# Thirteen matrix products of constants left out of TensorE's queue at three places of a two-block model

## The chip, the cores and the metric

One core of a Trainium2 chip runs one launch of the kernel. The metric is the device time of the launch in microseconds. An execution under the profiler gives the instructions with their times, counted from the first instruction.

## The reference

256 tokens of width 1024 in fp32 pass through a first model of two layers and then a second one of one layer. The first layer is a gated delta rule and a SwiGLU feed-forward; the second layer is an S5 state-space mixer with a gated output (GLU) and a mixture of eight experts, of which each token takes two. Cut to what surrounds the change:

```python
x = layer_norm(ALPHA * x + swiglu(x, ...), ...)          # end of layer 1
u = x @ s5_w_in                                           # entry to the second stage (S5)
...                                                       # state space, gelu
h = val * sigmoid(gate)                                   # halves of hid @ w_glu
x = layer_norm(ALPHA * x + h, ...)
logits = x @ w_router + b_router                          # routing: top 2 of 8
y = sum_e dense_gate[:, e] * swiglu_e(x)                  # experts
x = layer_norm(ALPHA * x + y, ...)
h = rmsnorm(x, norm_mix_g) ; proj = h @ w_in_2            # entry to the second block
```

## The kernel before

The kernel is written engine by engine: each engine's instructions stand in one hand-written order and meet through semaphores. No scheduler moves anything; what stands in TensorE's program runs in that order. Everything is fp32, and each product leaves two records in the profile, so that `keep_warm(bank, 3)` shows as six.

The 256 tokens are held as two tiles of 128 in `xres` (partition = token). After each layer norm, which VectorE computes tile by tile (`layer_norm`, `affine`, L1054 to L1059), TensorE turns the tile with eight transposes (`turn_x`, L2241 in the records), VectorE and ScalarE copy the result to `xT` (L822 and L1864), and TensorE waits for that (`need_x`) before it takes the next weight product.

`keep_warm` multiplies the identity by 512 columns of constants into a PSUM bank that nobody reads afterwards. It is called four times:

- `keep_warm(banks[0], 3)` behind the last feed-forward products (L2626) and the S5 kernel products (L2572), ahead of the second tile's transposes, which lead to the S5 input products (L2702, 256 products of 32 by 256);
- `keep_warm(banks[0], 5)` in the routing, behind the first tile's placement product (L2826) and ahead of the second tile's transposes. After these come the ones product (L2829), the first gather (L2820, eight products of 96 columns), the second tile's router (L2282, sixteen records of 8 columns) and the second gather;
- `keep_warm(banks[0], 1)` behind the placement products of the second tile (L2837, L2838) and ahead of the last sixteen records of gather, which wait for VectorE's selection (L1476, `pick`). VectorE copies their result (L1530), and the experts' up products (L2860) begin;
- `keep_warm(banks[6], 4)` behind the products that put the experts' outputs back in token order (L2899), ahead of the first tile's transposes and the second block's input products (L2282 with 512 columns, L2275).

Of the kernel before, what the change touches and what calls it, by code (L numbers as in the profile page):

```python
# [93 lines left out]
def build(nc, A, out):  # L94
    with ExitStack() as ctx:
# [14 lines left out]
        banks = [ctx.enter_context(nc.psum_tensor(f"bank{i}", [P, 512], F32)) for i in range(8)]  # L110
# [26 lines left out]
        def mat(i):  # L137
            return const[:, i, :]
# [2093 lines left out]
        def _(pe):  # L2232
# [10 lines left out]
            def keep_warm(bank, times):  # L2243

                for _ in range(times):
                    mm(bank[:, :], ident, const[:, 0:4].rearrange("p a b -> p (a b)"), start=True, stop=True)
# [3 lines left out]
            def turn_x(src, n, normed=None, at=None):  # L2250

                for j in (2 * n, 2 * n + 1):
                    if normed is not None:
                        pe.wait_ge(norm_done, 2 * normed + j + 1)
                    bank = at[j % 2] if at else banks[4 + j]
                    for i in range(4):
                        c = 4 * (j % 2) + i
                        last = transpose(four(bank)[:, i], src[:, n, P * c:P * c + P])
                    last.then_inc(xt_tr, 1)
                turned[0] += 1  # L2260
# [427 lines left out]
            for i in range(2):  # L2688
                s5_kernel(NPIECE - 1, i)
            pe.wait_ge(norm_v, 3)  # L2690
            keep_warm(banks[0], 3)
            turn_x(xres, 1, 2, (banks[4], banks[5]))
            need_x()

# [129 lines left out]
            pe.wait_ge(glu_read, nth_gv["c21", 0])  # L2824
            pe.wait_ge(chosen_ready, 1)
            mm(banks[1][:, 0:8], mat(C_TRI), chosen[:, 0], start=True, stop=True).then_inc(place_done, 1)  # L2826
            keep_warm(banks[0], 5)
            turn_x(xres, 1, 4, (banks[4], banks[5]))
            mm(banks[3][:, 0:16].rearrange("p (a b) -> p a b", a=2), mat(C_ONE), chosen[:, 0, None, :].broadcast_to((P, 2, 8)),  # L2829
               start=True, stop=False, skip_group_check=True)  # L2830
# [5 lines left out]
            pe.wait_ge(chosen_ready, 2)  # L2836
            mm(banks[3][:, 0:8], mat(C_TRI), chosen[:, 1], start=False, stop=True, skip_group_check=True)  # L2837
            mm(banks[3][:, 8:16], mat(C_ONE), chosen[:, 1], start=False, stop=True, skip_group_check=True).then_inc(place_done, 1)  # L2838
            keep_warm(banks[0], 1)
            for i in range(2):  # L2840
                gather(i, 1).then_inc(gath_done, 1)

# [52 lines left out]
            for n in range(NT):  # L2895
                for hf in range(2):
                    if hf == 1 and n == 0:
                        pe.wait_ge(m_yread_v, at(None, 1, 4))
                    mm(banks[2 * n + hf][:, :], back[:, P * n:P * n + P], y_turn[:, 512 * hf:512 * hf + 512], start=True, stop=True).then_inc(gath_done, 1)  # L2899
            keep_warm(banks[6], 4)  # L2900

            turn_x(xres, 0, 6)
            need_x()
# [250 lines left out]
```

## Time and profile before

| | us |
|---|---|
| median of 3 runs | 1252.93 |
| lowest, highest | 1251.98, 1253.33 |
| the profiled execution | 1258.34 |
| its span, first to last instruction | 1256.5 |
| TensorE busy in it | 1224.8 (97%) |
| VectorE, ScalarE busy | 609.6, 231.1 |

A row of the timeline gives the start in us, the time from the first start to the last end, engine, line, operation, written tile <- read tiles, the size of the weights, the size of the data, and how many records are merged in it; in brackets stands the idle time of the engine ahead of it and what ended it. PE is TensorE's products, PEld its weight loads, DVE is VectorE. A row of the windows gives a stretch, its length, the busy time with the number of instructions, the granted clock of TensorE as a share of 2.4 GHz, the share of time in which the DMA engines were busy, and GB/s.

### The profile page before, as it was taken

Reading aid. Unit: us, or ns where it says so; the run is one execution under the profiler, and the core shown is the slowest. Engines: PE = TensorE matmul, PEld = TensorE weight load, DVE = VectorE, ACT = ScalarE, POOL = GpSimd, SP = SyncE. Lnnn points to the kernel's source line nnn. Section 1 sums busy time; section 2 is a strip of 40 time slices with the busy share of each in tenths; the row PEclk is TensorE's granted clock in tenths of the full one; section 3 lists DMA queues with packets and bytes.
Section 4 is the critical chain, followed back from the end, with each engine's and each line's share of the span. In section 5 each row is a group of like instructions: output and inputs, shape, how many; then the busy total and the mean of one; then the engine's idle time right before and its main releaser. Section 6 shows DMA issues by size and latency. Waiting matters only on the chain.

```text
span 1256.5 us, 25396 instructions
## 1 busy us (share of the span) xinstructions
PE 1224.8 (97%) x11085; PEld 826.5 (66%) x11085; DVE 609.6 (49%) x1135; ACT 231.1 (18%) x487; POOL 100.9 (8%) x102
## 2 busy tenths in 40 slices
PE   8999999999999999999999999999999989999997
PEld 7878867899954467456545554555447547998443
DVE  1658445466898857663110111011174257656545
ACT  3362331222211104320100101010010032111000
POOL 1040024100000000002100000000143110000000
PEclk9999899999999999998999999999999999999999
DMA  9970804756554855629999999999996340535520
GB/s 329 358 247 2 268 1 102 170 152 181 156 205 172 157 88 188 265 103 404 405 407 416 417 407 407 419 412 406 376 330 209 121 148 1 191 145 194 187 88 33
DMA packets 121803, 291.09 MB, mean 232 GB/s; under 512 B 6324, under 2 KB 69280, under 8 KB 109440
## 3 DMA queue, kind: packets, MB, share of 16 engines
q1 hardware_dynamic: 109536, 269.30, 59.7%
q0 software_dynamic: 4832, 14.67, 4.0%
q10 hardware_dynamic: 7360, 6.03, 1.6%
q8 instruction: 57, 0.93, 0.3%
q14 instruction: 18, 0.15, 0.0%
HBM read 273.21 MB, written 16.78 MB: 231 GB/s over the span
## 4 chain that ended last, share of the span: by engine, by line
PE 92%; DVE 3%; ACT 2%; DMA 1%; issue 1%; SPq 0%; DVEq 0%; ACTq 0%
PE bank L2860 18%; PE bank L2619 10%; PE bank L2269 9%; PE bank L2877 9%; PE bank L3064 8%; PE bank L3102 7%; PE bank L2626 6%; PE bank L2282 5%; PE bank L2799 3%; PE bank L2241 3%; PE bank L2702 2%; PE bank L2951 1%; PE bank L2725 1%; DMA arena<-ffn_w 1%; PE bank L2471 1%
## 5 line engine op out<-in xcount | busy, mean ns | idle before, releaser
L2860 PE MATMUL bank<-arena 128*32 128x352 f32 x3072 | 230.4, 462 | 0.7 <-DVE arena L1530 0.7
L2860 PEld LDWEIGHTS bank<-arena 128*32 128x32 f32 x3072 | 104.1, 110 | 124.2 <-issue 123.0
L2269 PE MATMUL bank<-xT,arena 128*128 128x256 f32 x576 | 130.3, 386 | 1.3 <-ACT arena L1913 1.3
L2269 PEld LDWEIGHTS bank<-xT,arena 128*128 128x128 f32 x576 | 110.9, 195 | 17.0 <-ACT arena L1913 1.8
L1575 DVE TENSOR_TENSOR arena<-arena,bank 128x352 f32<-128x352 f32 x24 | 19.2, 801 | 204.4 <-PE bank L2860 204.4
L2877 PE MATMUL bank<-arena 128*32 128x256 f32 x2112 | 115.5, 379 | 0.0
L2877 PEld LDWEIGHTS bank<-arena 128*32 128x32 f32 x2112 | 70.8, 110 | 44.1 <-issue 2.2
L3102 PE MATMUL bank<-arena 128*128 128x512 f32 x224 | 96.7, 592 | 0.7 <-DVE arena L1727 0.7
L2619 PE MATMUL bank<-xT,arena 128*128 128x128 f32 x704 | 83.2, 275 | 0.5 <-DVE arena L1274 0.5
L2619 PEld LDWEIGHTS bank<-xT,arena 128*128 128x128 f32 x704 | 80.8, 192 | 2.0 <-issue 1.3
L2626 PE MATMUL bank<-arena 128*128 128x512 f32 x176 | 78.0, 594 | 0.0
L3102 PEld LDWEIGHTS bank<-arena 128*128 128x128 f32 x224 | 42.3, 190 | 53.6 <-issue 49.5
L2619 PE MATMUL bank<-arena 128*128 128x128 f32 x528 | 62.9, 276 | 2.0 <-issue 2.0
L2619 PEld LDWEIGHTS bank<-arena 128*128 128x128 f32 x528 | 60.7, 192 | 2.4 <-issue 2.3
L3064 PE MATMUL bank<-arena 128*128 128x128 f32 x512 | 58.5, 275 | 0.0
L3064 PEld LDWEIGHTS bank<-arena 128*128 128x128 f32 x512 | 57.8, 192 | 0.0
L2626 PEld LDWEIGHTS bank<-arena 128*128 128x128 f32 x176 | 32.4, 190 | 36.5 <-issue 36.5
L2799 PE MATMUL bank<-arena 128*128 128x512 f32 (+1 forms) x120 | 52.1, 598 | 2.7 <-issue 2.7
L3064 PE MATMUL bank<-xT,arena 128*128 128x128 f32 x384 | 44.6, 275 | 0.0
L3064 PEld LDWEIGHTS bank<-xT,arena 128*128 128x128 f32 x384 | 43.8, 192 | 1.0 <-issue 1.0
L2799 PEld LDWEIGHTS bank<-arena 128*128 128x128 f32 x120 | 24.3, 205 | 28.8 <-issue 27.9
L2138 ACT ACTIVATE arena<-bank,small 128x352 f32<-128x352 f32 x24 | 13.3, 555 | 156.8 <-PE bank L2860 156.8
(493 smaller groups left out, 1470.1 us busy)
## 6 DMA issues: line engine op xcount, KB each, us to landing
arena<-moe_w SPq DMA_DIRECT2D x64, 1408.0 KB, 16.1
arena<-moe_w SPq DMA_DIRECT2D x24, 1536.0 KB, 18.6
arena<-ffn_w SPq DMA_DIRECT2D x44, 512.0 KB, 6.6
arena<-w_up SPq DMA_DIRECT2D x8, 2048.0 KB, 9.4
arena<-w_down SPq DMA_DIRECT2D x8, 2048.0 KB, 7.6
arena<-gdn_w_in SPq DMA_DIRECT2D x7, 2048.0 KB, 18.7
arena<-ffn_w SPq DMA_DIRECT2D x11, 1024.0 KB, 4.9
slot_rows<-arena SPq DMA_DIRECT2D x1, 9600.0 KB, 54.0
```

The source lines that it names most:

```text
L1575: V_.tensor_tensor(mh[:, t].rearrange("p (x f) -> p f x", x=FE_T), msil[:, t].rearrange("p (f x) -> p f x", x=FE_T), banks[2 * t + 1][:, 0 ...
L2241: return nc.tensor.transpose(dst, src, const[0:k, C_ID, 0:k])
L2269: last = mm(bank[:, at:at + SEQ], w[:, k, P * m:P * m + P], x[:, k, :], start=(k == 0), stop=(k == KT - 1))
L2282: last = mm(bank, x[:, k0 + k, P * n:P * n + P], w[:, k], start=(k0 + k == 0), stop=(k0 + k == total - 1))
L2619: last = mm(bank[:, P * w:P * w + P], lhs[:, w, k], rhs[:, k], start=(i in ("1", "2", "5") and w == k == 0), stop=(k == 3), skip_group_che ...
L2626: last = mm(banks[2 * n + hf][:, :], f_tile(2 * c + k, n), f2[c][:, k, 512 * hf:512 * hf + 512], start=(c == 0 and k == 0), stop=(c == las ...
L2702: last = mm(banks[s // 2][32 * q:32 * q + 32, 256 * (s % 2):256 * (s % 2) + 256], x_sub[:, k, s], w[:, 256 * q:256 * q + 256], start=(k == ...
L2799: last = mm((bank or g_bank[h][i])[:, cols], lhs[:, k], rhs[:, k, cols], start=(k == 0 and i != 3), stop=(k == 3), skip_group_check=True)
L2860: last = mm(banks[i][32 * q:32 * q + 32, 0:EW1], xg[:, t, EK * s + kk], w[:, kk, EW1 * q:EW1 * q + EW1], start=(s == 0 and kk == 0), stop= ...
L2877: last = mm(y_bank[t][32 * q:32 * q + 32, 0:EW2], mhT[:, t, 32 * x:32 * x + 32], m2[c][:, x % 3, EW2 * q:EW2 * q + EW2], start=(x == 0), s ...
L3064: last = mm(bank[:, P * m:P * m + P], lhs[:, k, P * m:P * m + P], rhs[:, k], start=(i in (1, 2, 5) and m == k == 0), stop=(k == 3), skip_g ...
L3102: last = mm(d_bank[i][:, :], lhs[:, k], rhs[:, k], start=(d == k == 0), stop=(d == 7 and k == 1))
```

## The change

Four calls of `keep_warm` are left out, thirteen products in all. No other instruction, wait or transfer is changed; the queues of the other engines are the same, word for word.

```diff
@@ entry to the second stage
             pe.wait_ge(norm_v, 3)
-            keep_warm(banks[0], 3)
             turn_x(xres, 1, 2, (banks[4], banks[5]))
             need_x()
@@ routing
             mm(banks[1][:, 0:8], mat(C_TRI), chosen[:, 0], start=True, stop=True).then_inc(place_done, 1)
-            keep_warm(banks[0], 5)
             turn_x(xres, 1, 4, (banks[4], banks[5]))
...
-            keep_warm(banks[0], 1)
             for i in range(2):
                 gather(i, 1).then_inc(gath_done, 1)
@@ exit of the experts
-            keep_warm(banks[6], 4)
             turn_x(xres, 0, 6)
             need_x()
```

TensorE's queue at the entry to the second stage (L2572: S5 kernel products, L2241: transposes, L2702: input products):

```order
 L2626 MATMUL bank<-arena 128x512 x2
 L2572 MATMUL bank<-arena 32x128 x16
-L2246 MATMUL bank<-const 128x512 x3
 L2241 MATMUL bank<-const,xres 128x128 x8
 L2702 MATMUL bank<-arena,xT 32x256 x256
```

The transposes now stand straight behind the S5 kernel products. TensorE's queue in the routing, at the transposes of the second tile (L2826: placement of the first tile) and then at the last gather (L2837 and L2838: placement of the second tile):

```order
 L2799 MATMUL bank<-arena 128x256 x8
 L2826 MATMUL bank<-small,const 128x8
-L2246 MATMUL bank<-const 128x512 x5
 L2241 MATMUL bank<-const,xres 128x128 x8
 L2829 MATMUL bank<-small,const 128x16
...
 L2837 MATMUL bank<-small,const 128x8
 L2838 MATMUL bank<-small,const 128x8
-L2246 MATMUL bank<-const 128x512
 L2820 MATMUL bank<-arena,xres 128x96 x8
 L2844 TENSOR_LOAD passes
```

The transposes stand behind one product of 8 columns, and the last gather behind two. TensorE's queue at the experts' exit (L2899: outputs back in token order, L2282: input products of the second block):

```order
 L2898 REGISTER_ALU
 L2899 MATMUL bank<-arena 128x512 x3
-L2246 MATMUL bank<-const 128x512 x4
 L2241 MATMUL bank<-const,xres 128x128 x8
 L2282 MATMUL bank<-arena,xT 128x512 x8
```

The transposes now stand straight behind the products in token order.

## Rows read from the trace of the kernel before

**Rows 1.** The page: busy time of the engines, the chain's shares, the largest group.

```profile
PE 1224.8 (97%) x11085; PEld 826.5 (66%) x11085; DVE 609.6 (49%) x1135; ACT 231.1 (18%) x487; POOL 100.9 (8%) x102
...
PE 92%; DVE 3%; ACT 2%; DMA 1%; issue 1%; SPq 0%; DVEq 0%; ACTq 0%
...
L2860 PE MATMUL bank<-arena 128*32 128x352 f32 x3072 | 230.4, 462 | 0.7 <-DVE arena L1530 0.7
```

**Rows 2.** Windows of TensorE: stretch, length, busy (records), granted clock, DMA, GB/s.

```profile
504.20:507.50 3.30, 0.63 (x3) 1.00 0.04 16
507.80:510.90 3.10, 3.10 (x5) 0.50 0.00 0
...
558.90:562.10 3.20, 3.20 (x9) 0.50 0.00 0
...
572.60:579.20 6.60, 6.60 (x24) 0.50 1.00 400
...
582.90:586.00 3.10, 3.10 (x24) 0.50 0.96 410
...
434.00:446.00 12.00, 10.80 (x147) 1.00 0.88 157
926.00:941.00 15.00, 13.49 (x36) 1.00 1.00 278
```

**Rows 3.** Timeline, first GLU products, with two weight loads.

```profile
506.94 7.51 PE L2799 MATMUL bank<-arena 128*128 128x512 f32 x13 [2.67 <-issue]
...
508.14 0.34 PEld L2799 LDWEIGHTS bank<-arena 128*128 128x128 f32 x1 [0.51 <-issue]
...
511.72 0.19 PEld L2799 LDWEIGHTS bank<-arena 128*128 128x128 f32 x1 [0.24 <-issue]
```

**Rows 4.** Timeline of TensorE at the entry to the second stage.

```profile
431.60 1.04 PE L2241 MATMUL bank<-const,xres 128*128 128x128 f32 x8
...
435.30 2.84 PE L2246 MATMUL bank<-const 128*128 128x512 f32 x6
...
438.55 1.32 PE L2241 MATMUL bank<-const,xres 128*128 128x128 f32 x8 [0.41 <-DVE xres L1059]
...
440.65 5.63 PE L2702 MATMUL bank<-arena,xT 128*32 128x256 f32 x100 [0.78 <-DVE xT L822]
```

**Rows 5.** Timeline of TensorE in layer 1: eight transposes at half rate.

```profile
136.99 1.97 PE L2241 MATMUL bank<-const,arena 128*128 128x128 f32 x8
```

**Rows 6.** Timeline of TensorE at the experts' exit.

```profile
930.21 3.60 PE L2246 MATMUL bank<-const 128*128 128x512 f32 x8
...
933.65 1.30 PE L2241 MATMUL bank<-const,xres 128*128 128x128 f32 x8
...
935.78 7.11 PE L2282 MATMUL bank<-arena,xT 128*128 128x512 f32 x16 [0.83 <-DVE xT L1624]
```

**Rows 7.** Timeline of the routing, TensorE and VectorE's selection.

```profile
562.97 4.54 PE L2246 MATMUL bank<-const 128*128 128x512 f32 x10
...
567.67 1.32 PE L2241 MATMUL bank<-const,xres 128*128 128x128 f32 x8 [0.15 <-DVE xres L1059]
...
568.96 2.12 PE L2820 MATMUL bank<-arena,xres 128*128 128x96 f32 x8
...
570.91 2.08 PE L2282 MATMUL bank<-small,xT 128*128 128x8 f32 x16
...
572.85 2.17 PE L2820 MATMUL bank<-arena,xres 128*128 128x96 f32 x8
...
575.59 2.06 PE L2246 MATMUL bank<-const 128*128 128x512 f32 x2
...
575.97 0.27 DVE L1476 TENSOR_SCALAR arena<-const,small 128x96 f32<-128x96 f32 x1
...
577.43 3.85 PE L2820 MATMUL bank<-arena,xres 128*128 128x96 f32 x16
...
582.01 10.19 PE L2860 MATMUL bank<-arena 128*32 128x352 f32 x112 [0.73 <-DVE arena L1530]
```

## The prediction

> **What bounds the kernel now.** I read the page first: TensorE is busy for 97% of the span and makes up 92% of the chain that ended last, and in the largest group, the experts' up products, it idles for 0.7 us in all, released by VectorE and never by a transfer [rows 1]. So TensorE is the bound; a microsecond added to its queue ahead of the experts is found again at the end, since no transfer waits there to swallow it. Second I read the granted clock by stretches [rows 2]. The full rate is 2.4 GHz, and 0.50 is 1.2 GHz. The reader is to see that the clock is already lost now and then: TensorE idles for 2.67 us before the first GLU products [rows 3], keeps the full rate through that gap, and is at half rate from 507.8 to 510.9. It is at half rate again from 558.9 to 562.1 (after the router's products of 8 columns), from 572.6 to 579.2 (after the routing's thin products) and from 582.9 to 586.0 (just after the experts began). Over the two other places that the change touches, 434 to 446 and 926 to 941, it is 1.00 throughout [rows 2]. Third I read the instructions in order of time there.
>
> **What half rate costs.** A dense stretch pays in full: the fall at 507.8 is a stretch of about 3.4 us of half rate, in which dense products make half their way, so it costs 1.7 us. The weight loads slow as well: 0.34 us at 508.14, and 0.19 at 511.72 [rows 3]. Transposes, which are paced by their weight loads, do eight in 1.04 us at full rate [rows 4] and in 1.97 at half [rows 5].
>
> **The entry to the second stage.** Before: six records (three products) of 0.43 to 0.47 us fill 435.30 to 438.14, then 0.41 us of idle, then eight transposes, which VectorE's normalisation released, then 0.78 us of idle, then the stage's 512 input products [rows 4]. The fillers' end isn't late, so taking them out releases nothing earlier; it turns 0.41 us of idle into 3.25. The nearest row is the gap of 2.67 us, after which the clock fell [rows 3, 2]; this one is longer, so I take a fall as nearly certain. It comes near the gap's end, and what follows is transposes and a wait, not dense work. How long half rate then lasts has two bounds. Short: 3.4 us as at 507.8, of which 0.8 lies over the wait, leaving 2.6 us of half speed, 1.3 us. Long: 6.6 to 6.8 us as at 572.6, where the work after the fall was not dense either; less 0.8 of wait that is 6.0 us, 3.0 us, and with the transposes ahead of it slowed (0.4 us on the path, half of 1.97 less 1.04) 3.4 us. I take 2.3 us, the middle, since either is reached by where the fall lands. VectorE's copy between transposes and products doesn't depend on the clock.
>
> **The experts' exit.** The same figure in the same form: eight records from 930.21 to 933.81, transposes that start at 933.65, 0.83 us of idle, then 7.1 us of dense products [rows 6]. The fillers end just as the transposes start, so at most 0.2 us comes back. Without them TensorE idles for 3.3 us. Bounds 1.3 and 3.4 us, taken 2.3. The stage behind it is TensorE's too, so nothing gives this back.
>
> **The routing.** Ten records stand from 562.97 to 567.51; the transposes start at 567.67, 0.15 us of idle later, when VectorE's normalisation has ended [rows 7]. Without them the gap is 4.7 us and the fall comes in it or just behind it. Before, the full rate lasted until about 572.5. So what runs from 567.7 to 572.5 now runs at half rate:
> - eight transposes, in two lots released 0.66 us apart: 0.4 us more on the path (the second lot of four needs 0.9 instead of 0.5);
> - the first gather's eight products: 2.12 us at full rate, and the second's eight 2.17 at half, where they lie one after the other [rows 7]. They cost nothing;
> - the router's sixteen weight loads of 128 columns: 2.08 us now [rows 7]; at the half-rate transposes' pace of about 0.22 apiece 3.5, so 1.5 more. They gate VectorE's ranking and the gather behind them;
> - the filler between placement and gather: it runs at half rate, 2.06 us, and holds the last gather until 577.43. VectorE has written that gather's selection at 576.24 (575.97 + 0.27) [rows 7]; a weight load of 0.25 later the gather can start, at 576.5. That gives back 0.9 to 1.0 us.
>
> Sum 0.4 + 1.5 - 0.95 = 0.95, taken 1.0. Then the experts' entry: before, half rate lies on 3.2 us of it [rows 2], costing 1.7. After, half rate holds through the gather, and dense work must first bring the clock back; half rate then lies on 3.4 to 6.8 us of it, 1.7 to 3.4 us. Equally, another moment of the fall elsewhere may spare it. I count it as zero with bounds of -1.7 and +1.7.
>
> A rule of the Trainium skill would change this term. The traces show a 128-column load of 0.19 us at full rate and 0.34 at half [rows 3]. The page "TensorE: Matmul & The Clock Gate", section "LDWEIGHTS (loading the stationary operand)", gives the load's time as its columns over 1.2, with no clock in it. By that rule transposes and router keep their pace, and the routing comes to -0.95 instead of +1.0. The row speaks against it, and the sum goes by the row. The same page (section "What's actually happening") says that the moment of a change of rate depends on a free-running phase and so differs between runs of the same kernel; one trace can't show that.
>
> **Sum.** 2.3 + 1.0 + 2.3 = 5.6 us. The profiled execution takes 1258.34 us (span 1256.5 and 1.84 around it) and would become 1263.9; it stands 5.4 above the median of the runs, 1252.93, and the edits are the same in both, so the forecast is 1252.93 + 5.6 = 1258.5 us.
>
> **Rivals.**
> - **The gaps are harmless** (no difference). If the clock survives both gaps of about 3.3 us, only the routing is left, -0.95 to +1.0: 1252 to 1254. For it: the full rate held through the 2.67 us itself, and gaps of 0.4 and 0.8 us cost no clock [rows 2, 4]. Against it: the fall right behind the 2.67 us.
> - **Weight loads don't slow** (the skill's rule above, as a mechanism of this kernel: the routing's transposes and router are paced by loads that keep 0.1 us): 2.3 - 0.95 + 2.3 = 3.65, 1256.6. For it: the gather's equal pace at both rates. Against it: the transposes' 1.97 for 1.04.
> - **The filler in the chain was the only thing that counted** (faster). The last gather starts 0.95 us earlier, and the experts begin at another moment, at which half rate misses them: -1.7. Together -2.65: 1250.3. It decides only if both long gaps leave the clock alone and the routing's router isn't slowed, since each fall in a gap costs 1.3 or more. For it: the filler's 2.06 us do hold the gather [rows 7].
> - **Half rate lingers**. Both gaps at their long bound (3.4 each), the routing 1.0, and the experts' entry 1.7 more: 9.5, 1262.4. For it: the work behind each gap begins with transposes and a wait, and the stretch 572.6 to 579.2 shows that such work keeps half rate on.
>
> **How the numbers follow.** Forecast, all three places at the values taken, 1256.8 to 1261: 0.62. Lingering, 1261 to 1263.5: 0.13. Weight loads that don't slow, about 1256.6: 0.09. Harmless gaps, 1252 to 1254.5: 0.12. Faster, 1250.3: 0.04. The range of 8 in 10 reaches to 1255.0 below, which holds the rule of the weight loads and a case with one gap cheap, and to 1262.3 above, which holds most of the lingering. About 0.2%, 2.5 us, is what a measurement of this kernel can tell from no change. Slower than 1255.4: 0.62 + 0.13 + 0.09 = 0.84. Within: 0.12. Faster than 1250.4: 0.04.
>
> **What would show it.** In the profile after: a granted clock of 0.50 over some of 438 to 446 and of 934 to 943; the input products of the second stage losing 1 to 3 us to it; at the routing 0.50 from before the transposes on, the router's sixteen records at about 3.5 us instead of 2.08, and the last gather starting 0.3 us behind VectorE's selection. The prediction is wrong if the clock reads 1.00 behind the entry's or the exit's gap, if the router keeps its 2.1 us, or if a later wait shrinks by what was lost, which I rule out because TensorE waits for no transfer in the experts.

## The result, and the profile after

The changed kernel takes 1259.09 us (median of 20 runs, 1255.33 to 1263.05). The kernel before takes 1253.59 us (median of 20 runs, 1251.37 to 1257.79). The ratio is 1.0038, 95% interval 1.0030 to 1.0047: 4.8 us slower (3.8 to 5.9), where 5.6 was forecast. The 4.8 goes with the ratio and with the means of the two sets; the two medians stand 5.5 us apart. The profiled execution takes 1259.04 us, its span is 1257.2. One run of the kernel before, in the set beside the last three kernels below, took 2132.7 us at a granted clock of 0.555 and is left out of their comparison.

First the windows of TensorE after (stretch, length, busy with records, granted clock, DMA share, GB/s), to be held against [rows 2]:

```profile
434.00:440.30 6.30, 5.52 (x44) 0.50 1.12 181
440.80:446.00 5.20, 5.20 (x104) 1.00 0.60 118
...
505.60:508.60 3.00, 3.00 (x4) 0.50 0.00 0
553.00:558.00 5.00, 4.68 (x29) 1.00 0.58 248
...
563.60:583.80 20.20, 18.91 (x94) 0.50 1.00 414
584.10:590.00 5.90, 5.90 (x88) 1.00 0.89 349
...
932.20:938.70 6.50, 5.67 (x10) 0.50 1.05 245
939.10:943.00 3.90, 3.90 (x10) 1.00 1.03 258
```

Where the clock was 1.00 in [rows 2], at the entry and the exit, half rate now lies on 6.3 and 6.5 us. From the second tile's transposes in the routing to 4.6 us into the experts' products it lies on 20 us without a break. Then TensorE's timeline at the entry:

```profile
433.85 1.94 PE L2241 MATMUL bank<-const,xres 128*128 128x128 f32 x8 [3.27 <-DVE xres L1059]
436.57 29.80 PE L2702 MATMUL bank<-arena,xT 128*32 128x256 f32 x512 [0.78 <-DVE xT L822]
```

In [rows 4] the transposes took 1.32 us and the products began 2.10 us after them; here 1.94 and 2.72. Before, the 512 input products took, in the timeline:

```profile
440.65 27.86 PE L2702 MATMUL bank<-arena,xT 128*32 128x256 f32 x512 [0.78 <-DVE xT L822]
```

so the entry lost 0.6 us in the transposes and 1.9 in the products. TensorE's timeline in the routing after, against [rows 7]:

```profile
563.54 1.97 PE L2241 MATMUL bank<-const,xres 128*128 128x128 f32 x8 [4.59 <-DVE xres L1059]
...
565.59 2.18 PE L2820 MATMUL bank<-arena,xres 128*128 128x96 f32 x8
567.57 3.48 PE L2282 MATMUL bank<-small,xT 128*128 128x8 f32 x16
570.90 2.17 PE L2820 MATMUL bank<-arena,xres 128*128 128x96 f32 x8
...
574.35 4.14 PE L2820 MATMUL bank<-arena,xres 128*128 128x96 f32 x16 [0.56 <-DVE arena L1476]
```

and VectorE's selection in it:

```profile
574.03 0.27 DVE L1476 TENSOR_SCALAR arena<-const,small 128x96 f32<-128x96 f32 x1
```

The router's sixteen records take 3.48 us instead of 2.08, the first gather's eight records (four products of 96 columns, not eight as the text before says) 2.18 instead of 2.12, and the last gather starts 0.32 us behind the start of VectorE's selection (574.03), where it was 1.46 before. The timeline of the exit after, against [rows 6]:

```profile
931.46 1.78 PE L2241 MATMUL bank<-const,xres 128*128 128x128 f32 x8 [3.26 <-DVE xres L1059]
934.07 9.53 PE L2282 MATMUL bank<-arena,xT 128*128 128x512 f32 x16 [0.83 <-issue]
```

The second block's first sixteen records take 9.53 us instead of 7.11, and start 2.61 us behind the transposes instead of 2.13.

The two spans differ by only 0.7 us, and that must not be read as the price of the change. In us, from one fixed point to the next in either trace; the first of them is VectorE's last take of the feed-forward's result, before and after:

```profile
434.40 0.69 DVE L1040 SCALAR_TENSOR_TENSOR xres<-xres,bank 128x512 f32<-128x512 f32 x1 [0.86 <-PE bank L2626]
...
429.61 0.69 DVE L1040 SCALAR_TENSOR_TENSOR xres<-xres,bank 128x512 f32<-128x512 f32 x1 [0.87 <-PE bank L2626]
```

| stretch | before | after | difference |
|---|---|---|---|
| start to VectorE's last take of the feed-forward (L1040) | 434.40 | 429.61 | -4.8 |
| to the last S5 input product | 34.11 | 36.76 | +2.65 |
| first tile's router to the placement product (L2282 to L2826) | 7.03 | 5.34 | -1.7 |
| placement product to the experts' first product | 19.18 | 20.56 | +1.4 |
| the experts' first 384 up records | 30.30 | 30.93 | +0.6 |
| first product in token order (L2899) to the first L2275 product | 16.05 | 18.93 | +2.9 |

Four of the rows lie behind an edit: the input products, the stretch from the placement product to the experts, the experts' first products, and the exit. Together they lost 7.5 us. The trace of before carried two falls of the clock that this one lacks, and that no edit touches: 558.9 to 562.1 [rows 2], and 132.3 to 142.2, in the first layer; the window of before is:

```profile
132.30:142.20 9.90, 9.90 (x55) 0.50 1.06 279
```

Such falls come and go. Of the twelve traces of this document two have the one at 132; the one behind the first tile's router is in six of the ten kernels that have no filler there. That this is what spreads a kernel's runs over 6 to 8 us is borne out by the granted clock of each run: the fastest run of the changed kernel, 1255.33 us, had a mean of 0.984 and the slowest, 1263.05 us, 0.978, and over its twenty runs time and clock have a correlation of -0.92 (also -0.92 over 35 runs of the kernel before). So one pair of traces settles no total.

### The profile page after: what moved, and what is told of

It reads as the page before. It is cut to its first block, busy times and chain, and to the rows that moved or that the text cites. A ratio compares the mean times of both kernels' runs of the same rounds, so it can differ in the third digit from the quotient of the medians.

```text
span 1257.2 us, 25345 instructions
## 1 busy us (share of the span) xinstructions
PE 1215.4 (97%) x11059; PEld 805.4 (64%) x11059; DVE 612.6 (49%) x1135; ACT 231.3 (18%) x487; POOL 100.5 (8%) x102
## 4 chain that ended last, share of the span: by engine, by line
PE 92%; DVE 4%; ACT 2%; DMA 1%; issue 1%; SPq 0%; DVEq 0%; ACTq 0%
PE bank L2860 18%; PE bank L2619 10%; PE bank L2269 9%; PE bank L2877 9%; PE bank L3064 8%; PE bank L3102 7%; PE bank L2626 6%; PE bank L2282 5%; PE bank L2799 3%; PE bank L2241 3%; PE bank L2702 2%; PE bank L2951 1%; PE bank L2725 1%; DMA arena<-ffn_w 1%; PE bank L2471 1%
## 5 line engine op out<-in xcount | busy, mean ns | idle before, releaser
L2860 PEld LDWEIGHTS bank<-arena 128*32 128x32 f32 x3072 | 94.6, 111 | 134.3 <-issue 133.0
L2877 PEld LDWEIGHTS bank<-arena 128*32 128x32 f32 x2112 | 65.1, 110 | 49.9 <-issue 2.4
L2138 ACT ACTIVATE arena<-bank,small 128x352 f32<-128x352 f32 x24 | 13.3, 555 | 157.8 <-PE bank L2860 157.8
```

What stands on the lines that cost most here:

```text
L2860: last = mm(banks[i][32 * q:32 * q + 32, 0:EW1], xg[:, t, EK * s + kk], w[:, kk, EW1 * q:EW1 * q + EW1], start=(s == 0 and kk == 0), stop= ...
L2877: last = mm(y_bank[t][32 * q:32 * q + 32, 0:EW2], mhT[:, t, 32 * x:32 * x + 32], m2[c][:, x % 3, EW2 * q:EW2 * q + EW2], start=(x == 0), s ...
```

## The experiments

**Each place alone.** Four kernels, each with one of the four calls left out.

```diff
-            keep_warm(banks[0], 3)        # entry alone
```

> Only the three products at the second stage's entry are left out. Clock theory: TensorE falls to 1.2 GHz behind a gap of about 3.3 us, the transposes take 1.9 instead of 1.3 us, the S5 input products (27.9 us before) take 1.3 to 3 us more, and the kernel is 2.3 us slower (1.3 to 3.4). Rival, gap harmless: granted clock 1.00 from 434 to 446 and no difference in time (within 0.7 us). Rival, all of the loss sits in the routing: no difference either.

Measured 1.5 us slower (0.1 to 3.0). The windows of TensorE with the entry alone left out:

```profile
435.10:441.60 6.50, 5.72 (x50) 0.50 1.13 197
```

and in the timeline:

```profile
437.14 30.11 PE L2701 MATMUL bank<-arena,xT 128*32 128x256 f32 x512 [0.78 <-DVE xT L822]
```

The fall is there, and costs 2.3 us in the products of this trace and 0.4 in the way from the transposes to them. In the seven traces in which the entry's filler stands whole, the entry ran at 1.00. The harmless gap is ruled out at the entry.

```diff
-            keep_warm(banks[6], 4)        # exit alone
```

> Only the four products at the experts' exit are left out. Clock theory: half rate over the first tile's transposes and part of the second block's input products (7.1 us before becomes 8.6 to 10), kernel 2.3 us slower (1.3 to 3.4). Rival, gap harmless: clock 1.00 over 926 to 941, no difference. If the profile after is typical, 2.4 us in the products and 0.5 in the transposes: 2.9.

Measured 3.0 us slower (1.5 to 4.4). The timeline shows 8.96 us for the products that took 7.11, and they start 2.80 us behind the transposes instead of 2.13, so 2.5 us in all:

```profile
933.32 8.96 PE L2282 MATMUL bank<-arena,xT 128*128 128x512 f32 x16 [0.83 <-issue]
```

```diff
-            keep_warm(banks[0], 5)        # the routing's five alone
```

> Only the five products ahead of the second tile's transposes in the routing are left out; the one product behind the placement stays. Clock theory with slow weight loads: transposes 1.32 to 1.97, router 2.08 to 3.48, so 1.9 us slower, and up to 1.5 more where the experts begin at half rate for longer. Rival, weight loads keep their pace: within 0.5 us. Rival, the only place that matters: 4.8 us, the whole loss.

Measured 1.4 us slower (-0.4 to 3.1). The sign isn't settled by the time alone. The windows of its trace:

```profile
564.10:567.20 3.10, 3.10 (x16) 0.50 1.03 440
567.50:570.60 3.10, 3.10 (x24) 1.00 1.03 424
570.90:584.30 13.40, 12.67 (x65) 0.50 1.00 415
```

and the router in the timeline:

```profile
567.59 1.88 PE L2282 MATMUL bank<-small,xT 128*128 128x8 f32 x16
```

In this execution the clock came back for the 3.1 us in which the router ran, and the router took 1.88 us. In the trace of the whole change it didn't, and the router took 3.48. So the router's 1.4 us is a cost of some executions. With the five products in place it isn't free of it either: over the ten traces that have them the router took 1.88 to 2.70 us. What this trace saved on the router it paid in the experts, whose first 384 records took 30.30 us before:

```profile
578.60 31.47 PE L2859 MATMUL bank<-arena 128*32 128x352 f32 x384 [0.73 <-DVE arena L1530]
```

That is 1.2 us more, and from the placement product to the experts 19.73 us passed instead of 19.18: 1.7 us in all, near the 1.4 of the time and the 1.9 expected, but not at the place that was expected.

```diff
-            keep_warm(banks[0], 1)        # the one ahead of the last gather alone
```

> Only the one product between placement and last gather is left out. Chain theory: the last gather starts 0.25 to 0.4 us behind VectorE's selection instead of 1.2 us, so 0.95 us faster. Rival, the product kept the clock: without it half rate lies on 1 to 3 us more of the experts' first products than before, which takes 0.5 to 1.5 back, so between no difference and 0.5 slower.

Measured 0.4 us faster (2.0 faster to 1.1 slower): inconclusive. In the trace the last gather starts 0.33 us behind the selection's start (570.95), so the chain is shorter by 1.1 us at this place. The time can't tell how much of that the clock took back. In this trace it was 0.4: from the last gather to the experts 4.87 us pass instead of 4.58, and the experts' first 384 records take 30.38 instead of 30.30, which leaves 0.8 faster. Half rate lay on 13.3 us here, into the experts, by the windows:

```profile
566.30:579.60 13.30, 12.01 (x60) 0.50 1.01 414
```

and the last gather in the timeline:

```profile
571.28 4.14 PE L2820 MATMUL bank<-arena,xres 128*128 128x96 f32 x16 [0.56 <-DVE arena L1476]
```

The four add up to 5.5 us, within the interval of the whole change. The exit is the dearest place, and no one place holds all of it.

**Busy, but narrow.** At entry and exit the wide products give way to narrow ones that keep TensorE busy for the same time.

```diff
+                    mm(bank[:, 0:8], ident, const[:, 0, 0:8], start=True, stop=True)     # keep_thin
...
-            keep_warm(banks[0], 3)
+            keep_thin(banks[0], 12)
...
-            keep_warm(banks[6], 4)
+            keep_thin(banks[6], 14)
```

> At entry and exit the fillers are kept in time but not in width: 12 and 14 products of the identity by 8 columns stand where 3 and 4 products by 512 columns stood (about 2.9 and 3.4 us either way, by the router's 0.12 us a record). The routing is as before. Theory of the work done: TensorE is busy through both gaps and the clock falls all the same, so the loss of entry and exit together, 4.5 us (3.5 to 5.5). Rival, only idleness lowers the clock: no fall over 434 to 446 and 926 to 941, no difference.

Measured 7.0 us slower (5.1 to 8.9). TensorE's timeline (the helper moves lines by five):

```profile
431.37 2.85 PE L2251 MATMUL bank<-const 128*128 128x8 f32 x24
434.62 1.97 PE L2241 MATMUL bank<-const,xres 128*128 128x128 f32 x8 [0.40 <-DVE xres L1059]
437.37 29.59 PE L2707 MATMUL bank<-arena,xT 128*32 128x256 f32 x512 [0.78 <-DVE xT L822]
```

and its windows:

```profile
434.30:440.80 6.50, 5.40 (x41) 0.50 1.05 187
...
932.60:939.00 6.40, 5.53 (x13) 0.50 1.04 229
```

The exit's products in the timeline:

```profile
935.43 9.02 PE L2287 MATMUL bank<-arena,xT 128*128 128x512 f32 x16 [0.83 <-issue]
```

The idle time ahead of the entry's transposes is 0.40 us, as in [rows 4], TensorE counts as busy for the 2.85 us before, and yet the clock is at half rate from 434.3 to 440.8. So idleness as such isn't the cause: with products of 8 columns in the same time the clock fell as with an empty gap, with products of 512 columns it held. Other widths were not tried.

**Both gaps empty**, beside it.

```diff
-            keep_warm(banks[0], 3)
...
-            keep_warm(banks[6], 4)
```

> The products at the entry and at the exit are both left out, those of the routing stay. It stands beside the kernel in which narrow products fill the same two gaps (7 us slower, 5.1 to 8.9). Theory, only the lost width counts: the same loss, between the sum of the single removals (4.5 us) and 7. Rival, narrow products do harm of their own beyond the clock: 4.5 us or less here.

Measured 5.6 us slower (3.8 to 7.5). The interval overlaps that of the narrow products, and it holds both what the theory and what the rival expected, so the time decides nothing between them. The timeline does, as far as one trace can:

```profile
437.19 29.50 PE L2701 MATMUL bank<-arena,xT 128*32 128x256 f32 x512 [0.78 <-DVE xT L822]
...
934.16 9.47 PE L2282 MATMUL bank<-arena,xT 128*128 128x512 f32 x16 [0.83 <-issue]
```

With the way from the transposes to the products counted in, entry and exit lost 5.1 us here and 5.0 with the narrow products. So those are worth as much as nothing, and harm of their own isn't shown; why their time came out above the 3.5 to 5.5 expected stays open. It also leaves little for the routing: with both gaps empty and the routing as before the kernel is as slow as the whole change (4.8), within the intervals.

**Shorter gaps.**

```diff
-            keep_warm(banks[0], 3)
+            keep_warm(banks[0], 2)
...
-            keep_warm(banks[6], 4)
+            keep_warm(banks[6], 2)
```

> Two products instead of three at the entry and two instead of four at the exit, so gaps of about 1.3 and 1.8 us. Theory: a gap of this size is less than the 2.67 us behind which the clock fell in the trace of before, so the full rate holds in most runs and the time is within 1 us of before; if shorter gaps cost as the whole ones do, 4.5 us slower.

Measured 0.9 us slower (-0.4 to 2.3). In its trace the exit kept the full rate, and the entry did not. The timeline at the entry:

```profile
434.78 1.32 PE L2241 MATMUL bank<-const,xres 128*128 128x128 f32 x8 [1.26 <-DVE xres L1059]
```

and in the windows:

```profile
437.30:440.40 3.10, 3.10 (x36) 0.50 1.14 243
...
924.00:940.00 16.00, 12.82 (x35) 1.00 0.98 277
```

A gap of 1.26 us, transposes and a wait of 0.78 were enough here for one short stretch of half rate. I had expected full rate in most runs; one trace can't say how often it falls, but the time says that it costs less than the whole gaps.

**More fillers.** If the cause is right, the falls that the trace of before shows can be bought off too.

```diff
             pe.wait_ge(e_read, 8)
+            keep_warm(banks[0], 3)
             pe.wait_ge(hid_ready, 12)
```

> The kernel before with one addition: three products of constants in the 2.67 us ahead of the first GLU products. Clock theory: the fall behind that gap, 1.7 us of loss in the traces that show it, goes: 1.5 us faster (1 to 2). Rival: the added 2.6 us end behind the wait and hold the GLU products: no difference or slower.

Measured 1.5 us faster (3.4 faster to 0.4 slower): the size that was expected, its sign just not settled. The fall behind the gap of [rows 3] is gone, and the clock is at 1.00 over the whole stretch to the routing, by the windows:

```profile
497.00:568.00 71.00, 69.54 (x277) 1.00 0.59 230
```

All nine traces without this filler have a fall there, and none of the three with it. That the fall at 558.9 is missing too isn't the filler's doing as far as is known: it is also missing in the trace of the whole change and in two others.

Together with one product ahead of the first tile's router, and without the one ahead of the last gather:

```diff
             pe.wait_ge(e_read, 8)
+            keep_warm(banks[0], 3)
             pe.wait_ge(hid_ready, 12)
...
             glu_product(7, 1)
+            keep_warm(banks[0], 1)
             need_x()
...
-            keep_warm(banks[0], 1)
             for i in range(2):
                 gather(i, 1).then_inc(gath_done, 1)
```

> The one product between placement and last gather is left out, and fillers are added at two other gaps: three products in the 2.67 us ahead of the first GLU products, one in the 0.97 us ahead of the first tile's router. Clock theory: the falls at 507.8 and at 558.9 go, each 1.7 us where it occurs, and the last gather starts 0.95 us sooner: 2 to 3.5 us faster. Rival: fillers end later than the waits they fill, or the falls come elsewhere: no difference to 1 us slower.

Measured 2.6 us faster than the kernel before (1.1 to 4.0), ratio 0.9979, interval 0.9968 to 0.9991. The added products fit their waits: in the timeline 0.17 us of idle is left behind the three. What the one ahead of the router brings isn't settled, since the fall behind the router comes and goes without it.

```profile
500.56 2.74 PE L2246 MATMUL bank<-const 128*128 128x512 f32 x6
503.47 8.85 PE L2800 MATMUL bank<-arena 128*128 128x512 f32 x20 [0.17 <-issue]
```

Its windows:

```profile
497.00:567.00 70.00, 69.38 (x271) 1.00 0.58 228
568.00:578.00 10.00, 8.70 (x48) 0.50 1.01 419
```

The last addition goes into the wait between the last gather and the experts:

```diff
                 gather(i, 1).then_inc(gath_done, 1)
+            keep_warm(banks[0], 1)
```

> The fastest kernel so far (2.6 us faster than before) with one more product of constants behind the last gather, in the 0.73 us in which TensorE waits for VectorE's copy of the gathered tokens. Theory: the clock is back earlier in the experts' first products, up to 1.7 us less half rate, and at half rate the filler ends 1 us late: 2 to 4 us faster than before. Rival: the filler's overhang costs more than the clock gives: 1.5 to 2.5 us faster than before.

Measured 5.3 us faster than the kernel before (3.4 to 7.0), ratio 0.9958, interval 0.9944 to 0.9973, the fastest of all: median 1248.65 where before stood at 1253.91 on the same chip. Its timeline at the experts' entry:

```profile
575.26 1.97 PE L2246 MATMUL bank<-const 128*128 128x512 f32 x2
577.16 29.37 PE L2862 MATMUL bank<-arena 128*32 128x352 f32 x384
```

where the kernel without that filler has:

```profile
574.12 30.56 PE L2861 MATMUL bank<-arena 128*32 128x352 f32 x384 [0.73 <-DVE arena L1530]
```

The windows with the filler:

```profile
568.70:578.60 9.90, 9.33 (x40) 0.50 1.00 410
```

The filler runs at half rate, covers the wait and ends 1.0 us behind it: VectorE's copy ends at 576.07, and the experts begin at 577.16, where without the filler they began 0.1 us behind that copy. Of the 9.9 us at half rate only 1.4 lie on the experts' products here, where 3.9 did without it (experts from 574.12, half rate to 578.0). The two kernels were compared with before in separate sets of runs, and their intervals overlap, so how much of the 2.7 us between them this one filler brings isn't settled by the time. In the two traces it brings 0.2: 1.2 us less in the experts' first 384 records, 1.0 more ahead of them. So most of the 2.7 is not explained by it, and may be chance.

## Why the prediction was right, step by step

- **Bound and carrying through.** Right. The loss of the entry and of the exit came out at the end: both gaps alone make the run 5.6 us longer (3.8 to 7.5), and the two stages of its trace lost 5.1.
- **Entry, 2.3 taken, 1.3 to 3.4.** The fall came with the gap, 6.3 us of half rate. The traces show 2.65 us in the whole change and 2.6 when only the entry is emptied; the time says 1.5 (0.1 to 3.0). Right in mechanism and inside the range. The stretch was of the long form, for which 3.4 us was reckoned; it cost less because the fall came ahead of the transposes, so that some 2.6 of its 6.3 us lay on them and on the wait, and only the rest on dense products (1.9 us lost). The transposes cost 0.6, where 0.4 was reckoned.
- **Exit, 2.3 taken.** 2.9 us in the trace, 3.0 (1.5 to 4.4) by the time. The term was somewhat small: half rate lay on 6.5 us, again the long form, and cost 2.4 us in the products and 0.5 ahead of them, between the middle and the bound of 3.4.
- **Routing, 1.0 taken.** In the trace after 1.4: transposes to gather 0.8 (0.4 was taken; the ones product between them slowed as well), router 1.4 (1.5 taken), the first gather less than 0.1 and the second nothing, placement to last gather -1.1 (-0.95 taken), and the last gather's own stretch up to the experts 0.3, which I had left out. By the time, the two routing edits alone give 1.4 and -0.4, together 1.0, each with an interval as wide as itself. The router's part holds only where half rate lasts, as the kernel without the routing's five shows; there the loss lay in the experts instead.
- **Experts' entry, 0 taken, -1.7 to 1.7.** 0.6 us more in this pair of traces and 1.2 with the five alone left out, inside the bounds, but not zero in either.
- **Weight loads that don't slow.** Ruled out for the router and the transposes: the router's sixteen loads of 128 columns take 3.48 us at half rate and 1.88 at full (the 2.08 of [rows 7] ends behind the fall at 572.6). The Trainium skill's formula in "TensorE: Matmul & The Clock Gate", section "LDWEIGHTS (loading the stationary operand)", has no clock in it; the measurement decides against it here. The gather kept its pace, 2.18 for 2.12, as its row of before said.
- **Harmless gaps, faster, lingering.** Harmless gaps are ruled out by every trace that has gaps of 3.3 us: the clock fell behind all six. The faster case needed harmless gaps. Lingering did occur in the trace (20 us of half rate through the routing, 0.6 us more in the experts), and both gaps had the long form; together the places cost 7.5 us in the trace, not the 9.5 of that rival, because much of the half rate lay on waits, transposes and gathers.
- **The sum.** 5.6 against 4.8 (3.8 to 5.9). The profiled pair gives 7.5. Part of the excess can be the router: before's took 2.08 us in this pair, up to 2.70 in other traces with the same routing, and without the five products 3.48 or 1.88. At entry and exit nothing of the kind was seen: wherever the fillers stand whole the clock read 1.00, in seven traces each. The rest of the way from 7.5 to 4.8 stays open.
- **What was luck.** By the time, the two gaps alone cost 5.6 us (3.8 to 7.5), where 4.6 was taken, and the whole change, with the routing's edits on top, 4.8. So the gaps' terms look small and the routing's +1.0 looks large; the intervals are too wide to say so, but the closeness of 5.6 to 4.8 may owe something to two errors of opposite sign.

## What to carry to other kernels

A wait in front of dense TensorE work can cost more than its length: after two waits of 3.3 us each this kernel lost 1.5 to 3 us more behind each, because the products that follow run at 1.2 GHz. Fill such a wait with products of full width (512 columns) that end just before the releaser; products of 8 columns keep the engine busy and the clock falls all the same, and a filler that ends behind its wait costs its overhang (1.0 us of the 1.2 gained, at the experts' entry). Look first for short waits that nobody filled: the 2.67 us ahead of the GLU products lost the clock in all nine traces. Where runs of one kernel spread by the clock, read the price stage by stage from fixed points, and take the total from many runs.

## What the runs showed of the hardware

- The clock fell behind gaps of 3.3 us (six of six), 2.67 us (nine of nine traces; none of three once it was filled) and, with transposes and another short wait behind it, 1.26 us (one trace). It also fell with TensorE busy but for 0.40 us, with products of 8 columns.
- Weight loads of 128 columns slow at half rate: 0.22 us apiece in the router against 0.12. The gather's loads, also of 128 columns but eight elements apart in memory, come every 0.25 us at either rate (eight in 1.98 us at full, in 2.01 at half).
- Stretches of half rate that no edit touches come and go: 132.3 to 142.2 in before's trace and 131.9 to 141.7 in the fastest kernel's, and the window of the change from 120 to 145 is at 1.00:

```profile
120.00:145.00 25.00, 24.82 (x408) 1.00 0.71 188
```

What decides in which executions a fall lands there, no run here settles.
